# Token rows of each expert gathered on chip by products with 0/1 slot tables, in place of a scatter to memory and loads of rows

## The reference

```python
def moe_ffn(x, w_router, b_router, w1, w3, w2):
    logits = (x @ w_router + b_router).astype(jnp.float32)
    top_v, top_i = lax.top_k(logits, TOP_K)          # TOP_K = 2 of N_EXPERTS = 8
    top_w = jax.nn.softmax(top_v, axis=-1)
    gate = jnp.sum(jax.nn.one_hot(top_i, N_EXPERTS) * top_w[..., None], axis=-2)
    out = gate[..., 0:1] * swiglu(x, w1[0], w3[0], w2[0])
    for e in range(1, N_EXPERTS):
        out = out + gate[..., e:e + 1] * swiglu(x, w1[e], w3[e], w2[e])
    return out
```

## Time and profile before

| | us |
|---|---|
| median of three runs | 2375.5 |
| lowest and highest of them | 2374.35, 2380.61 |
| the profiled execution, its own time | 2378.48 |
| its span | 2376.7 |
| TensorE busy in the span | 2199.9 (93%) |
| VectorE, ScalarE, GpSimd busy | 724.2, 634.9, 580.6 |
| bytes moved by DMA | 521.24 MB |

### The profile page before, as it was taken

The page is one execution under the profiler, slowest core; times in us unless marked ns, Lnnn a source line. Parts: engine busy times, 40 slices in busy tenths (PEclk is TensorE's granted clock), DMA queues, the critical chain, the costliest instruction groups (busy, mean ns, idle before and its releaser), DMA issues.

```text
span 2376.7 us, 58172 instructions
## 1 busy us (share of the span) xinstructions
PE 2199.9 (93%) x26470; PEld 1417.8 (60%) x26470; DVE 724.2 (30%) x1428; ACT 634.9 (27%) x966; POOL 580.6 (24%) x390
## 2 busy tenths in 40 slices
PE   6999898889999999979779888999999999999995
PEld 3676677667777877867567775444444444333352
DVE  2047766633233223351865533000000000000002
ACT  3243554434222222254455532010000000000002
POOL 5333544343343433434353440000000000000000
PEclk7999899989999999989889997999999999999997
DMA  7732001224635455333000129999999999999993
GB/s 286 257 124 80 7 4 39 90 89 136 218 122 192 161 183 189 103 121 108 2 7 4 39 72 388 399 408 398 403 403 395 402 404 404 387 402 408 408 395 134
DMA packets 186034, 521.24 MB, mean 219 GB/s; under 512 B 7728, under 2 KB 74432, under 8 KB 179136
## 3 DMA queue, kind: packets, MB, share of 16 engines
q1 hardware_dynamic: 175664, 487.48, 54.4%
q10 hardware_dynamic: 8976, 25.87, 3.4%
q0 software_dynamic: 1152, 4.19, 0.5%
HBM read 496.15 MB, written 21.36 MB: 218 GB/s over the span
## 4 chain that ended last, share of the span: by engine, by line
PE 45%; issue 39%; DVE 8%; ACT 4%; DMA 2%; POOL 1%; SPq 0%; POOLq 0%; DVEq 0%; ACTq 0%
PE bank L331 10%; PE bank L333 10%; PE bank L332 10%; PE bank L2145 2%; PE bank L2141 2%; PE bank L2156 2%; PE bank L1997 1%; DVE arena L1651 1%; PE bank L2118 1%; POOL w_lo L321 1%; PE bank L2127 1%; DMA arena<-in_w_in_dram 1%; ACT arena L1392 1%; ACT w_hi L315 1%; PE bank L2198 1%
## 5 line engine op out<-in xcount | busy, mean ns | idle before, releaser
L321 POOL TENSOR_TENSOR w_lo<-arena,w_hi 128x2048 fp32r<-128x2048 f32 (+1 forms) x77 | 349.9, 4544 | 571.7 <-ACT w_hi L315 571.7
L876 PE MATMUL bank<-arena 128*32 128x512 f32 (+1 forms) x3680 | 445.4, 556 | 0.6 <-ACT arena L622 0.6
L331 PE MATMUL bank<-h_hi,w_hi 128*128 128x512 f32 (+1 forms) x1008 | 390.3, 387 | 28.0 <-DVE h_lo L1562 13.6
L333 PE MATMUL bank<-h_hi,w_lo 128*128 128x512 f32 (+1 forms) x1008 | 376.8, 374 | 0.0
L332 PE MATMUL bank<-h_lo,w_hi 128*128 128x512 f32 (+1 forms) x1008 | 376.8, 374 | 0.0
L879 PE MATMUL bank<-arena 128*32 128x256 f32 (+1 forms) x3680 | 265.8, 360 | 0.0
L879 PEld LDWEIGHTS bank<-arena 128*32 128x32 f32 x3680 | 119.6, 110 | 241.0 <-issue 227.3
L331 PEld LDWEIGHTS bank<-h_hi,w_hi 128*128 128x128 f32 x1008 | 194.7, 193 | 90.3 <-issue 35.6
L950 PE MATMUL bank<-arena 128*32 128x512 f32 (+1 forms) x2208 | 220.0, 555 | 11.0 <-DMA arena<-in_moe_w_dram 5.3
L606 POOL DMA_INDIRECT arena<-slot_y,arena x4 | 3.8, 950 | 879.8 <-ACTq L698 878.9
L332 PEld LDWEIGHTS bank<-h_lo,w_hi 128*128 128x128 f32 x1008 | 194.8, 193 | 35.6 <-issue 4.6
(11 more groups left out here) (303 smaller groups left out, 2707.2 us busy)
## 6 DMA issues: line engine op xcount, KB each, us to landing
arena<-in_moe_w_dram SPq DMA_DIRECT2D x168, 2048.0 KB, 15.9
arena<-in_w_mod_dram SPq DMA_DIRECT2D x48, 1024.0 KB, 5.2
arena<-in_ffn_w_dram SPq DMA_DIRECT2D x42, 1024.0 KB, 7.5
arena<-in_w_in_dram SPq DMA_DIRECT2D x26, 1024.0 KB, 7.0
arena<-in_w_out_dram SPq DMA_DIRECT2D x8, 1024.0 KB, 9.5
slot_x<-arena ACTq DMA_DIRECT2D x14, 384.0 KB, 3.4
slot_y<-arena ACTq DMA_DIRECT2D x14, 384.0 KB, 5.0
x_store<-arena ACTq DMA_DIRECT2D x2, 2048.0 KB, 8.4
```

The lines of the kernel that those rows point to most:

```text
L321: eng.tensor_tensor(lo, slot_view(splits[i][0]), hi, ALU.subtract).then_inc(sem("w_lo"), 1)
L331: nc.tensor.matmul(out_, ah, bh, start=(first and i == 0), stop=False)
L333: ins = nc.tensor.matmul(out_, al, bh, start=False, stop=(last and i == n - 1))
L876: mm(bank[b][64 * h + 32 * c:64 * h + 32 * c + 32, 0:n // 2], xa[:, 32 * c:32 * c + 32], w[:, n // 2 * h:n // 2 * (h + 1)], start=first, s ...
```

## The change

The rows of every item, and of the trio, are now gathered as those of item 0 were: by float32 products of `XTK` with a 0/1 table. VectorE makes the table of the next item inside each item (`pick`, `pick_trio`), after its first multiplication. `slot_x`, its zeroing, the four scatters, the wait for them, the loads of rows, and `XR` and `XRS` are gone. TensorE waits for `m_pick` (the table) where it waited for `m_xr` (the rows).

```diff
-        slot_x = nc.dram_tensor("slot_x", [n_slots, D], fp32).ap()
...
-        SEL = area(o_m + 2304, 2, SLOTS)
-        XRS = area(o_hb, 2, D)
+        SEL = area(o_m + 3840, 2, SLOTS)
+        SEL_S = area(o_m + 4032, 2, 256)
...
-            for n in range(2):
-                for t in range(2):
-                    at = bass.IndirectOffsetOnAxis(ap=slot_i[:, 2 * n + t:2 * n + t + 1], axis=0)
-                    nc.gpsimd.indirect_dma_start(slot_x, at, XTK[:, t], None).then_inc(sem("slot_x"), 16)
...
-            def rows(i):
-                act.dma_start(XR, slot_x.rearrange("(i s) d -> i s d", s=SLOTS)[bass.ds(i, 1)][0]).then_inc(sem("m_xr"), 16)
...
-            def rows_trio():
-                act.dma_start(XRS, slot_x[S_AT:S_AT + 256, :].rearrange("(t p) d -> p t d", p=P)).then_inc(sem("m_xr"), 16)
...
-            act.wait_ge(sem("slot_x"), 64)
+            act.wait_ge(sem("slot_0"), 1 + 16 * NS)
...
+            for h in range(2):
+                ts(rel_s[:, h], slot_f, -float(S_AT + P * h), None, ALU.add)
+            nc.vector.tensor_copy(rel, slot_f).then_inc(sem("m_pick"), 1)
...
+            def is_slot(dst, at, n, t):
+                if n == 0:
+                    return ts(dst, io[:, 0:dst.shape[-1]], at[:, t:t + 1], None, ALU.is_equal)
+                return stt(out=dst, in0=io[:, 0:dst.shape[-1]], scalar=at[:, 2 + t:3 + t], in1=dst, op0=ALU.is_equal, op1=ALU.add)
+
+            def pick(i):
+                dve.wait_ge(sem("m_pick"), 3 * i + 1)
+                ts(rel, rel, -float(SLOTS), None, ALU.add).then_inc(sem("m_pick"), 1)
+                for n in range(2):
+                    dve.wait_ge(sem("m_pick"), 3 * i + n + 2)
+                    for t in range(2):
+                        ins = is_slot(SEL[:, t], rel, n, t)
+                    ins.then_inc(sem("m_pick"), 1)
...
-            def item(i):
+            def item(i, more):
                 for s in range(NC):
                     dve.wait_ge(sem("m_sig"), NC * i + s + 1)
                     for src, cols in spans(0, s):
                         ins = tt(SGM[:, cols], SGM[:, cols], src, ALU.mult)
                     ins.then_inc(sem("m_s"), 1)
+                    if s == 0 and more:
+                        pick(i)
+                    elif s == 0:
+                        pick_trio(i)
...
-            def gather(i):
-                pe.wait_ge(sem("m_xr"), 16 * i)
+            def gather():
                 for r in range(2):
                     for k in range(4):
-                        c = (4 * r + k) * P
-                        ins = nc.tensor.transpose(pk(r, 4, SLOTS)[:, k], XR[:, c:c + P], ident[0:SLOTS, 0:SLOTS])
+                        for t in range(2):
+                            ins = mm(pk(r, 4, SLOTS)[:, k], XTK[:, t, (4 * r + k) * P:(4 * r + k + 1) * P], SEL[:, t],
+                                     start=(t == 0), stop=(t == 1))
                     ins.then_inc(sem("m_ga"), 1)
...
                 if more:
-                    gather(i + 1)
+                    pe.wait_ge(sem("m_pick"), 3 * i + 4)
+                    gather()
                 else:
-                    gather_trio(i)
+                    pe.wait_ge(sem("m_pick"), 3 * i + 3)
+                    gather_trio()
                 down(i, NC - 1)
 
-            def gather_trio(i):
-                pe.wait_ge(sem("m_xr"), 16 * i + 16)
+            def gather_trio():
                 for r in range(4):
                     for k in (2 * r, 2 * r + 1):
                         for t in range(2):
-                            ins = nc.tensor.transpose(pk(r, 2, 256)[:, k % 2, t * P:(t + 1) * P],
-                                                      XRS[:, t, k * P:(k + 1) * P], ident)
+                            ins = mm(pk(r, 2, 256)[:, k % 2], XTK[:, t, k * P:(k + 1) * P], SEL_S[:, t],
+                                     start=(t == 0), stop=(t == 1))
                     ins.then_inc(sem("m_ga"), 1)
...
-                            for rows in (slot_x, slot_y):
-                                act.dma_start(rows[SLOTS * g:SLOTS * (g + 1), :], area(o_mix, D)[0:SLOTS]) \
-                                   .then_inc(sem("slot_0"), 16)
+                            act.dma_start(slot_y[SLOTS * g:SLOTS * (g + 1), :], area(o_mix, D)[0:SLOTS]) \
+                               .then_inc(sem("slot_0"), 16)
```

More of the change, by code:

```diff
@@ L418, in hybrid_kernel @@
         slot_i = table(4).bitcast(i32)
+        rel = table(4)
+        rel_s = table(2, 4)
         io_i = table(P).bitcast(i32)
@@ L437, in hybrid_kernel @@
         XG = area(o_m + 3072, KD, SLOTS)
-        XR = area(o_m + 3840, D)[0:SLOTS]
         YG = area(o_mix, 2, 2, D)
-        SEL = area(o_m + 2304, 2, SLOTS)
-        XRS = area(o_hb, 2, D)
+        SEL = area(o_m + 3840, 2, SLOTS)
+        SEL_S = area(o_m + 4032, 2, 256)
         XGS = area(o_hb + 2 * D, KD, 256)
@@ L595, in moe_pool @@
             pool.wait_ge(sem("slots"), 1)
-            pool.wait_ge(sem("xtk"), 4)
-            pool.wait_ge(sem("slot_0"), 1 + 32 * NS)
-            for n in range(2):
-                for t in range(2):
-                    at = bass.IndirectOffsetOnAxis(ap=slot_i[:, 2 * n + t:2 * n + t + 1], axis=0)
-                    nc.gpsimd.indirect_dma_start(slot_x, at, XTK[:, t], None).then_inc(sem("slot_x"), 16)
             pool.wait_ge(sem("slot_y"), 1)
@@ L669, in item @@
                         gate_rows(i, s - 1)
[L670 to L673, removed]
                 gate_rows(i, NC - 1)
@@ L804, in item_trio, with pick_trio @@
                         times(g, s).then_inc(sem("m_g"), 1)
-            def item(i):
+            def is_slot(dst, at, n, t):
[10 more added lines that the diff above has]
+                    ins.then_inc(sem("m_pick"), 1)
+            def pick_trio(i):
+                for n in range(2):
+                    dve.wait_ge(sem("m_pick"), 3 * i + n + 1)
+                    for t in range(2):
+                        for h in range(2):
+                            ins = is_slot(SEL_S[:, t, P * h:P * h + P], rel_s[:, h], n, t)
+                    ins.then_inc(sem("m_pick"), 1)
+            def item(i, more):
                 for s in range(NC):
@@ L819, in moe_dve @@
             with dve.Fori(0, last) as i:
-                item(i)
-            item(last)
+                item(i, True)
+            item(last, False)
             item_trio()
@@ L1150, in _ @@
             for l in range(L):
-                wait(pool, *(("xT", KD) if l == 0 else ("slot_0", 1 + 32 * NS)))
+                wait(pool, *(("xT", KD) if l == 0 else ("slot_0", 1 + 16 * NS)))
                 nc.gpsimd.memset(w2z, 0.0).then_inc(sem("zeroed"), 1)
```

## The result

| | before | changed |
|---|---|---|
| median of four runs, us | 2376.69 | 2394.18 |
| lowest to highest | 2374.35 to 2380.61 | 2392.58 to 2394.70 |
| profiled execution: span | 2376.7 | 2390.8 |

The ratio is 1.0065, with a 95% interval of 1.0048 to 1.0083: slower by 15 us (11 to 20); the two medians lie 17.5 us apart. The forecast was 16.4 us more, 2391.9 us in a range of 2386 to 2397, worked out from a median of 2375.5 for the kernel before. With its fourth run that median is 2376.69.

The account below looks back on a forecast made before the run. TensorE was taken to bound the kernel up to 2100, then DMA to the end. Gathers of items +11.3 and of the trio +5.1, all else 0, sum to +16.4 us: 2375.5 becomes 2391.9 us, range 2386 to 2397.

Parts of the forecast that it names:

- TensorE sets the pace in the items: Items before the trio: TensorE has no gap and weight loads wait for it, so its time counts in full.
- The gathers of the items, +11.3: Items 1 to 4: 32 records at 0.112 us, 3.57 us per gather instead of 0.75, adding 11.3 us in all.
- The trio's gather, +5.1: Trio's start: 32 records at 0.216 us, 6.91 us instead of 1.84, adding 5.1 us; bounds +1.7 and +8.7.
- The transfers, 0: Scatters and row loads before 2016, 4.72 MB or 11.7 us at 402 GB/s: removing them gains 0.
- DMA's chain from 2100 to the end: Trio: DMA restarts at 2100 when TensorE releases its place, then works without pause and sets the end.
- the second rival: Trio: DMA enters ahead and TensorE's 5.3 us of waits for weights go, giving 2386.6 us; chance 0.08.
- The cut at 2100: Trio: no DMA backlog at 2100; the unit issued at 2100.8 started only when TensorE released its place, landing after 9.1 us.
- The tables and ScalarE's wait, 0: Inside items and trio: VectorE's tables (1.3 and 2.2 us) are covered, and ScalarE starting some 6 us earlier gains 0.
- DMA as the pace: Items: rival that DMA sets the pace, so saved transfers count 11.7 us, giving 2363.8 us; chance 0.05.
- No wait for `m_pick`: Five gathers: the rival claimed TensorE waits some 1 us at each for table, bank or copy, 2397 us; chance 0.07.
- a product has two records: Gathers: forecast counted 32 records for 16 products; the rival claimed one record each, 2381.3 us; chance 0.02.
- A sign of my own: Start of the trio: the prediction is wrong if it moves by less than 16 us.

Follow-up runs that it names:

- late bytes: Changed kernel with four more 1 MB loads (4.19 MB) issued by ScalarE in chunks 1 and 2 of the trio, which nobody reads: 2406.98 us, ratio 1.0126.
- even order: Kernel before and changed kernel, each with the trio's units of A, B, C in turn and B/C's turn right behind A's: 2375.55 us and 2392.01 us.
- transposes: Changed kernel with the gathers of items 1 to 4 and trio as transposes of on-chip rows, no row transfers: 2376.04 us, ratio 0.9999.
- late turns: Changed kernel with the twelve transposes of expert A's turn of chunk 1 in the trio done four times: 2393.56 us, ratio 1.0073.
- fp32r: Changed kernel with token rows as two fp32r tiles and fp32r tables, each float32 product becoming two fp32r products: 2392.22 us, ratio 1.0083.
- transfers back: Changed kernel with the zeroing, the four scatters, ScalarE's wait and the loads of rows put back, all products kept: 2395.75 us, ratio 1.0077.
- trio by transposes: Changed kernel with only the trio's gather as sixteen transposes of on-chip tokens, the items' gathers still products: 2390.39 us, ratio 1.0066.
- no tables: Changed kernel without the tables VectorE makes inside the items; all products still run, on old table contents: 2394.85 us, ratio 1.0085.
- gather twice: Changed kernel with the sixteen products of each gather at the ends of items 1 to 4 issued twice: 2408.38 us, ratio 1.0136.

## Why the prediction was right

**TensorE sets the pace in the items.** Shown by three runs: twice the products make the items stretch 14.3 us longer for 14.3 us of work, the transfers put back leave it at 580.5, and taking them away without the products leaves it at 563.8 (ratio 0.9999).

**The gathers of the items, +11.3.** 3.64 us each against 3.57 forecast and 0.75 before: +11.6. The 0.07 is the step from the last product to the next matmul, which is longer than a pitch and which my count of 32 pitches left out.

**The trio's gather, +5.1.** 7.01 against 6.91: +5.2. The rows at 1387, of the same form, were the right ones. By the factor of four for float32 transposes in the Trainium skill, TensorE: Matmul & The Clock Gate, section Terms, my estimate would have been 6.0 and 14.7 us; the trace has 3.64 and 7.01.

**The transfers, 0.** Right. The forecast that the DMA share would fall below 1 was wrong in form: it reads 1.00 to 1.02 without the transfers. What fell was GB/s (402 to 389) and the time to landing (15.6 to 10.3 us); not 9.1, as I had it, since two issues overlap. The share seems to count time with packets under way, which would stay full while two loads overlap; that was not tested.

**DMA's chain from 2100 to the end.** Right in what it said of this change: late TensorE work is free (a trio of 313.4 us against 314.4 with 3.9 us more work in it, waits down from 5.2 to 0.8) and late bytes are paid (10 us for 4.19 MB). The waits in the trio stayed, 5.3 and 5.2, so the second rival fell. The cut at 2100 itself matters less than I thought: the even order gains 1.8 us in the kernel before and 3.4 in the changed one.

**The tables and ScalarE's wait, 0.** Right, by the run without tables and by ScalarE's start some 6 us earlier, which moved nothing.

**The rivals.** DMA as the pace, with the page on the most-contended engine behind it (the Trainium skill, Perfetto Trace Analysis, section Identifying the Most-Contended Engine), fell by the run with transposes. There, as in the kernel before, the weight-load share, one of the two measures that the section wants for TensorE, is 44% (246.26 of 556.00 us) beside a DMA share of 1.02, and TensorE is the pace all the same. No wait for `m_pick` shows, and a product has two records.

**A sign of my own that came out against me.** I wrote that the prediction is wrong if the start of the trio moves by less than 16 us. It moved by 2034.1 - 2021.4 = 12.7. The sign was badly built: it counts from the start of the span, so it takes in the first stretch, which differs by -3.9 us. Counted from item 0 the trio starts 16.7 us later.

The sum of the profile, 16.7 + 0.8 + 0.5 - 3.9 = +14.1, holds three terms that I had at nothing. The -3.9 of the first stretch is not shown to be the change's. The dense channel mixer, where the zeroing lay, takes the same time: 1500 matmuls from 623.6 to 952.2 us of the kernel before take 328.6 us in its trace and in those of all the other kernels here, with the zeroing and without. The changed kernel was 2.7 us ahead before that place. Such leads come in steps of 1 to 2 us in the dense part; at one of them the granted clock differs (window, the kernel before and then the changed one):

```profile
374.00:377.00 3.00, 3.00 (x60) 2.36 (x59) 1.83 (x5) 1.20 (x2) 0.00 (x0) 0.50 0.00 0
374.00:377.00 3.00, 2.76 (x90) 2.36 (x92) 2.49 (x7) 1.19 (x2) 0.00 (x0) 1.00 0.00 0
```

The kernel before with the even order has the same dense part as the kernel before, and it reaches item 0 at 1455.1 in place of 1457.5. All the kernels reach it between 1451.3 and 1460.0, and with the zeroing the run with the transfers put back does so at 1457.2. The other three stretches alone make +18.0, beside 17.5 between the medians, where I had 16.4. Of the 1.6 us that I missed, 0.3 is the gathers, 0.8 the trio's half clock (last section), and 0.5 the rest, which varies between 41.7 and 43.5 us over all the kernels.

## What to carry to other kernels

Two resources that both read as full are told apart by who waits for whom and by a fixed pitch of the one's instructions, not by either share: here DMA stood at 1.03 and 402 GB/s and yet 4.7 MB less were worth nothing. Then price a change by place: in a stretch that TensorE paces, its microseconds count in full and bytes for nothing, and in the next stretch, where DMA has the pace, it is the other way round. A gather by 0/1 products had a floor here: every record with a new block of 128 x 128 took 0.11 us at the least, with 96 columns in either type, and there were two records for each of two token tiles. A transpose of rows that a DMA has placed had one record where the products have four.

## What the runs showed of the hardware that I had not expected

A wait of TensorE for weights can cost more than its length: the clock fell behind some of them. In the changed kernel's trio TensorE waited 3.48 us from 2312.5, and a stretch at half clock follows; the group of 192 records then takes 12.12 us where the same kind of group before it takes 10.57 (timeline, then the window 2312 to 2320 with its granted clock of 0.79):

```profile
2298.46 10.57 PE L964 MATMUL bank<-arena 128*32 128x256 f32 x192 [0.20 <-DMA arena<-in_moe_w_dram]
2308.82 3.70 PE L971 MATMUL bank<-arena 128*32 128x128 f32 x128
2316.01 12.12 PE L964 MATMUL bank<-arena 128*32 128x256 f32 x192 [3.48 <-DMA arena<-in_moe_w_dram]
```

```profile
2312.00:2320.00 8.00, 4.52 (x68) 2.51 (x63) 0.42 (x1) 0.38 (x1) 0.00 (x0) 0.79 1.05 387
```

The kernel before had 2.68 us at the same place, and the next group at 10.57. The half clock accounts for the trio's lengths in the order of before. Where no group shows it (the kernel before, transposes, late turns, fp32r) the trio takes 313.0 to 313.6 us. Where one is some 1.5 us longer (changed, transfers back, trio by transposes, no tables) it takes 314.2 to 315.0, and 316.0 where the group takes 13.38 us (gather twice). So the 0.8 and 1.6 us by which the trio grew are most likely the clock's.

The length of the wait does not decide it. In the fp32r kernel a wait of 3.53 us, as long as the changed kernel's, is followed by full clock, and in the changed kernel with the even order one of 2.74 us is followed by half clock:

```profile
2314.81 10.57 PE L972 MATMUL bank<-arena 128*32 128x256 f32 x192 [3.53 <-DMA arena<-in_moe_w_dram]
2252.63 12.09 PE L961 MATMUL bank<-arena 128*32 128x512 f32 x96 [2.74 <-DMA arena<-in_moe_w_dram]
```

(The second is a group that takes 10.51 us at full clock.) And at 1910 in the fp32r kernel the clock fell with no wait ahead of it, behind a gather. What brings it on stays open; no run here tried it by itself.
